# A gate with tokens on partitions, softmax divisions at the place of their transposes, a bias and a sum moved, in a streamed-weight transformer kernel

## Chip, core and metric
One core of one Trainium2 chip runs the whole kernel. The metric is the device time in microseconds (us) of one execution; the time before is the median of three runs.

## The reference
256 tokens with 1024 channels in float32 run through three kinds of block. First two layers of a mixing block and a feed-forward; the mixing block has four branches:

```
h = rms_norm(x, g_mix[l]);  proj = h @ w_in[l]
y_a = dsa_attention(qa, ka, va, qi, ki, iw) @ w_oa[l]      # softmax over the 64 best keys of an indexer
y_b = silu(layer_norm(causal_dwconv(glu))) @ w_ob[l]
y_c = (gb * causal_dwconv(gc * xc)) @ w_oc[l]
y_d = stick_breaking_attention(sq, sk, sv) @ w_od[l]
merged = gates[0] * y_a + gates[1] * y_b + gates[2] * y_c + gates[3] * y_d
x = x + merged @ w_merge[l]
x = x + (silu(causal_dwconv(h2 @ w_ffn_gate[l])) * (h2 @ w_ffn_up[l])) @ w_ffn_down[l]
```

Then two layers of a hybrid block, with latent attention (MLA, 4 heads), a gated delta rule (GDN, 4 heads of 128, chunks of 64) and block attention with a position bias (MoBA):

```
beta = sigmoid(b);  g = -exp(A_log) * softplus(a + dt_bias)      # b, a: 4 + 4 columns of the input product
gc = cumsum(g in a chunk);  decay = exp(gc_i - gc_j)
q, k, v = silu(causal_conv(qkv));  q, k normed
L = strict(beta * k k^T * decay);  W, U0 = (I + L)^-1 [k beta exp(gc), v beta]
A = q k^T * decay;  o = scan over chunks of the state
mla: softmax(q k^T + causal) v;  moba: softmax(q k^T * scale + t5_bias) v
```

and a last norm.

## The kernel before
Every engine runs a program written out by hand, in which a step waits on semaphores and raises one; `Values` keeps which count belongs to which value. Weights come in parts of 1024 columns by 128 partitions (four to a column group), streamed by one queue into `ring` (three slots). For each part ScalarE (ACT) writes the rounded high half `whi` (`split_hi`, L1250), VectorE (DVE) the low half `wlo` = weight - high (`split_lo`, L1884), and TensorE (PE) computes high times high, high times low halves (L525, L547, L614) and then low times high (L534, L555, L636). DVE and ACT split part j + 4 while PE is at part j. PSUM has eight banks; main products rotate over four ("m"), side products over the other four ("s"), and `Banks.take` waits until the previous owner's readers have left.

All else is side work. It is written as generators (`sparse_p`, `decay_v`, `delta_a` and so on: `_p` on PE, `_a` on ACT, `_v` on DVE) that are run at places of the tables MIX_PLAN and TWO_PLAN. Place 2j of a stage is, on PE, between the high and the low products of part j, and place 2j + 1 behind them; on ACT and DVE place 2j is ahead of the split of part j + 4, and 2j + 1 behind it. The stages in order: two layers of mixing and feed-forward, then the hybrid stage "two", layer 0 in about 969 to 1147 us, layer 1 from there to the end.

The parts that the change touches:
- Softmax: `logits_v` (masks and scales the products, L2001, maxima at L2005) waits for ACT's exponentials (L1316) and divides (L2008 reciprocal, L2010 product). PE then transposes the quotients (L504, `cst` is the identity), four blocks for token block 0 and eight for block 1. It runs for sparse attention in the mix layers, for MLA and for MoBA in the hybrid ones.
- The delta gate: `ba_p` multiplies the 8 gate columns (stationary, L896) with all 256 tokens; `ba_a` copies the 8 rows out of PSUM (L1615), `decay_p` transposes them, `decay_v` (L2446 to L2473) and `decay_a` (L1621 to L1640) make beta, the log decays, their sums and the decay matrix `Dm`. Ahead of the sums, `awake` puts six products of ones on PE (L499).
- The keys' convolution: `two_a` copies one half of the channel products (L1787), `two_v` adds the other (L2715), then `four_taps` (L2426) on DVE and ACT (L1780).
- The norm squares of keys and queries: ACT squares at L1704, and PE sums over channels (the x16 products with one column, L499 `onesb,w`).
- The queries' scores A, step 1 of `others`; T_, the update of the block solve of the delta rule, L2611 and L2616 on DVE, with Mm as its matrix buffer.
- The position bias: `bias_p`, four products with a flip matrix, and `bias_v`, copies and the causal mask, in layer 0 of the hybrid stage.
- MoBA's output neighbours: DVE's L2649 to L2656 norm the delta output and take their root from GpSimd (POOL, L2772).

Of the kernel before, what the change touches and what calls it, by code (L numbers as in the profile page):

```python
# [7 lines left out]
F32R = mybir.dt.float32r  # L8
# [5 lines left out]
P = 128  # L14
# [59 lines left out]
def two0(l):  # L74
# [14 lines left out]
        "stick": [100, 105, 107, 113],  # L89
# [92 lines left out]
def build(nc, a, out):  # L182
    ctx = ExitStack()
    with ctx:
# [23 lines left out]
        wba = sb("wba", [P, 64])  # L208
        bhi = sb("bhi", [P, 64], F32R)
        blo = sb("blo", [P, 64], F32R)  # L210
# [23 lines left out]
        def part2(o, n):  # L234
            return w2[:, o:o + n]
# [33 lines left out]
        def cols(h):  # L269
# [43 lines left out]
        rows8 = part2(23040, S)[0:8]  # L313
# [26 lines left out]
                                              bufH[:, 0:512]))  # L340
# [153 lines left out]
        def tensor(e):  # L494
# [108 lines left out]
            def chans_first(j, held_of, name, l, mid, after):  # L603
# [17 lines left out]
                for i in range(4):  # L621
# [5 lines left out]
                    products(i, 0, (2, 3))  # L627
                for i in range(4):
# [215 lines left out]
            def ffn_p(l):  # L844
# [35 lines left out]
            def bias_p(l):  # L880
                for h in range(4):
                    yield h
                    bk = ps.take(e, "s", "bias", h)
                    e.wait_ge(DMA["bi"], 64)
                    e.wait_ge(DMA["fl"], 16)
                    group(bk[:, 0:S], [(flipB, toepB[:, h * S:(h + 1) * S])]).then_inc(*up("bias.p"))
                    put("bias.p", "bias", h)

            def ba_p(l):
                yield 1  # L890
                bk = ps.take(e, "s", "ba", l)
                wh, wl = (b[:, :].rearrange("p (k n) -> p k n", k=8) for b in (bhi, blo))
                e.wait_ge(*at("ba", "lo", l))
# [4 lines left out]
                done.then_inc(*up("ba.p"))  # L898
                put("ba.p", "ba", "done", l)

            def decay_p(l):
                yield 0
# [2116 lines left out]
```

## Time and profile before
| | |
|---|---|
| time, median of three runs | 1321.51 us (1320.49 to 1323.34) |
| profiled execution | 1323.16 us, span 1321.4 us |
| PE busy | 1295.2 us, 98% |
| DVE busy | 1037.0 us, 78% |
| ACT busy | 734.9 us, 56% |
| POOL busy | 49.3 us, 4% |
| HBM read | 223.49 MB, 170 GB/s over the span |

The span runs from the first to the last instruction of one execution. A timeline row of the section of rows below gives the start in the span, the time the group took, the engine, the line, the operation, output and input by the program's names, the form of one, how many, and in brackets the engine's idle time ahead of it with what ended it. Where a group holds both an engine's and another's rows, the rows are of two timelines. Granted clock is TensorE's, as a share of full speed.

### The profile page before, as it was taken

The page shows a single profiled execution, that of the slowest core. Times are in us where ns is not written, and L with a number is a line of the kernel's source. Part 1 is how long each engine was busy: PE and PEld are TensorE (multiplying, and loading weights), DVE is VectorE, ACT ScalarE, POOL GpSimd, SP SyncE. Part 2 cuts the span into 40 slices and gives each one's busy share as a digit, 9 for nine tenths or more (in the row PEclk, how much of TensorE's full clock was granted, in tenths as well). Part 3 has the DMA queues.
Part 4 walks back from the last instruction along what each step waited for, and adds up shares of the span by engine and source line. Part 5 has one row for each costly group of instructions (what it writes and reads, how often), then busy time and mean ns, then how long its engine had stood idle before and what let it go on. Part 6 is the DMA issues. An engine that isn't in the chain of part 4 may idle for free.

```text
span 1321.4 us, 26181 instructions
## 1 busy us (share of the span) xinstructions
PE 1295.2 (98%) x10716; PEld 1233.1 (93%) x10716; DVE 1037.0 (78%) x1733; ACT 734.9 (56%) x1087; POOL 49.3 (4%) x48
## 2 busy tenths in 40 slices
PE   8999999999999999999999999999999999999998
PEld 8899999999999989999999999999989899898997
DVE  7999998678877677999997778777777846787565
ACT  6554566555454455544747565454557546585364
POOL 0000000000000000000000000000001100001100
PEclk9999999999999999999999999999999999999999
DMA  8565455565555457655355547665653224433232
GB/s 297 189 200 183 160 162 184 167 223 202 197 192 191 152 200 232 210 163 202 125 207 166 198 150 252 211 206 180 208 184 128 65 97 130 141 125 111 81 103 74
DMA packets 109711, 226.23 MB, mean 171 GB/s; under 512 B 6260, under 2 KB 17780, under 8 KB 109592
## 3 DMA queue, kind: packets, MB, share of 16 engines
q1 hardware_dynamic: 104656, 218.91, 49.6%
q10 hardware_dynamic: 4936, 5.65, 1.3%
q8 instruction: 85, 1.39, 0.4%
q14 instruction: 34, 0.28, 0.1%
HBM read 223.49 MB, written 1.06 MB: 170 GB/s over the span
## 4 chain that ended last, share of the span: by engine, by line
PE 78%; DVE 13%; ACT 3%; issue 3%; DMA 2%; POOL 0%; SPq 0%; POOLq 0%; DVEq 0%; ACTq 0%
PE bank L525 29%; PE bank L534 15%; PE bank L547 11%; PE bank L499 7%; PE bank L555 6%; DVE wlo L1884 4%; PE bank L586 3%; PE bank L504 2%; DMA ring<-in_w_in 2%; DVE w L2085 2%; PE bank L593 2%; DVE w L2426 1%; PE bank L614 1%; ACT whi L1250 1%; PE bank L636 1%
## 5 line engine op out<-in xcount | busy, mean ns | idle before, releaser
L1250 ACT ACTIVATE whi<-ring 128x1024 fp32r<-128x1024 f32 (+3 forms) x428 | 431.3, 1024 | 329.2 <-PE bank L525 194.9
L1884 DVE TENSOR_TENSOR wlo<-ring,whi 128x1024 fp32r<-128x1024 f32 (+3 forms) x428 | 495.8, 1184 | 147.9 <-ACT whi L1250 121.6
L525 PE MATMUL bank<-hboth,whi 128*128 128x256 f32 x3648 | 452.1, 277 | 1.3 <-DVE w L2715 1.3
L525 PEld LDWEIGHTS bank<-hboth,whi 128*128 128x128 f32 x3648 | 430.4, 193 | 3.6 <-issue 2.2
L534 PE MATMUL bank<-hboth,wlo 128*128 128x256 f32 x1824 | 247.4, 277 | 0.0
L534 PEld LDWEIGHTS bank<-hboth,wlo 128*128 128x128 f32 x1824 | 223.3, 192 | 3.8 <-issue 3.2
L547 PE MATMUL bank<-whi,hboth 128*128 128x512 f32 (+2 forms) x448 | 98.8, 363 | 0.0
L2085 DVE SCALAR_TENSOR_TENSOR w<-w,par 128x256 f32<-128x256 f32 x240 | 98.0, 478 | 0.0
L499 PE MATMUL bank<-w 64*64 64x64 f32 (+6 forms) x1312 | 88.3, 245 | 3.0 <-DVE w L2611 2.4
L547 PEld LDWEIGHTS bank<-whi,hboth 128*128 128x128 f32 x448 | 80.3, 189 | 9.3 <-issue 0.9
L499 PEld LDWEIGHTS bank<-w 64*64 64x64 f32 (+3 forms) x1312 | 73.6, 148 | 11.0 <-DVE w L2550 2.8
L2772 POOL TENSOR_TENSOR st<-st,mhalf 128x1 f32<-128x1 f32 (+2 forms) x34 | 36.2, 1064 | 1174.0 <-DVE st L1905 540.6
L614 PE MATMUL bank<-hboth,whi 128*128 128x256 f32 x384 | 52.2, 283 | 3.5 <-DVE hboth L1912 2.5
L547 PE MATMUL bank<-whi,fhi 128*128 128x512 f32 x144 | 54.6, 379 | 0.0
L547 PE MATMUL bank<-whi,flo 128*128 128x512 f32 x144 | 54.6, 379 | 0.0
L555 PE MATMUL bank<-wlo,hboth 128*128 128x512 f32 (+2 forms) x224 | 53.9, 363 | 0.0
L614 PEld LDWEIGHTS bank<-hboth,whi 128*128 128x128 f32 x384 | 47.0, 188 | 6.5 <-DVE hboth L1912 3.5
L555 PEld LDWEIGHTS bank<-wlo,hboth 128*128 128x128 f32 x224 | 40.7, 189 | 4.3
L1263 ACT ACTIVATE sgb<-x 128x512 f32<-128x512 f32 x28 | 17.6, 628 | 38.3 <-DVE x L1899 35.9
L1586 ACT ACTIVATE fhi<-w 128x512 fp32r<-128x512 f32 x22 | 13.9, 630 | 41.9 <-DVE w L2395 41.9
L555 PE MATMUL bank<-wlo,fhi 128*128 128x512 f32 x144 | 37.0, 379 | 0.0
L2382 DVE SCALAR_TENSOR_TENSOR w<-w,par 128x256 f32<-128x256 f32 x88 | 36.7, 478 | 0.0
(315 smaller groups left out, 1555.8 us busy)
## 6 DMA issues: line engine op xcount, KB each, us to landing
ring<-in_w_in SPq DMA_DIRECT2D x100, 1024.0 KB, 5.1
ring<-in_w_ffn_down SPq DMA_DIRECT2D x22, 1024.0 KB, 5.1
ring<-in_w_ffn_gate SPq DMA_DIRECT2D x20, 1024.0 KB, 5.1
ring<-in_w_ffn_up SPq DMA_DIRECT2D x20, 1024.0 KB, 5.1
ring<-in_w_merge SPq DMA_DIRECT2D x8, 1024.0 KB, 5.0
ring<-in_w_out SPq DMA_DIRECT2D x8, 1024.0 KB, 5.0
ring<-in_w_oc SPq DMA_DIRECT2D x4, 1024.0 KB, 5.2
ring<-in_w_od SPq DMA_DIRECT2D x4, 1024.0 KB, 5.1
```

Of the source, the lines that this page charges most:

```text
L499: done = e.matmul(o, l_, r_, start=start and i == 0, stop=stop and i == len(pairs) - 1)
L525: done = e.matmul(o, wh[:, k, cols(u)], paired(s_[:, k0 + k, :]), stop=False, skip_group_check=True, start=opens and k == 0 and s_ is sh a ...
L534: done = e.matmul(o, wl[:, k, cols(u)], paired(sh[:, k0 + k, :]), start=False, stop=closes, skip_group_check=True)
L547: done = e.matmul(held[u][:, 0:n], s_[:, k0 + k, cols(u)], paired(wh[:, k, 0:n]), stop=False, start=opens and k == 0 and s_ is sh, skip_gr ...
L555: done = e.matmul(held[u][:, 0:n], sh[:, k0 + k, cols(u)], paired(wl[:, k, 0:n]), start=False, stop=closes, skip_group_check=True)
L586: done = e.matmul(acc[nh][tb][:, :], s_[:, k0 + k, cols(tb)], paired(wh[:, k, :]), start=False, stop=False, skip_group_check=True)
L614: done = e.matmul(held[u][:, tb * S:tb * S + S], wh[:, k, cols(u)], hboth[:, :, 2 * i + k, cols(tb)], start=i == 0 and k == 0 and tb == 0, ...
L1250: e.activation(part_of(whi, j), part_raw(j), ACT.Copy).then_inc(*up("hi.a"))
L1884: e.tensor_tensor(part_of(wlo, j), part_raw(j), part_of(whi, j), ALU.subtract).then_inc(*up("lo.v"))
L2085: e.scalar_tensor_tensor(out=cacc[:, c], in0=glup[:, c, j:j + S], scalar=wv, in1=cacc[:, c], op0=ALU.mult, op1=ALU.add).then_inc(*up(name))
L2382: e.scalar_tensor_tensor(out=y, in0=g, scalar=wv, in1=y, op0=ALU.mult, op1=ALU.add).then_inc(*up("ffn.v"))
L2772: e.tensor_tensor(dst, src, half(n), ALU.pow).then_inc(*up(name))
```

## The change
Its parts:
1. The delta gate is computed with the tokens on partitions: `ba_products` uses the activations (128 tokens) as stationary and the 8 gate columns, high and low halves side by side in `bhl`, as moving side, 16 products for each token block. Block 0's run behind its first products of the keys' part, block 1's at place 5. DVE's `tensor_reduce` sums the parts straight out of PSUM. The copy of the rows, their transposes and the six idle products go. The decay's places are 5, 6, 7, 8, and the gate columns are split ahead of the norm.
2. The keys' high copy and sum are ahead of the split of the part that follows (`kc`, i == 3).
3. The position bias is computed in the last feed-forward, two banks and four DVE operations.
4. The division is a function `probs_v` of its own. Block 0's runs behind block 1's logits; block 1's at the place of PE's transposes: step 14 (place 146) for sparse attention, step 7 (place 41) for MLA, step 11 (place 63) for MoBA.
5. The queries' scores go from place 32 to 36; `Mm` has another buffer, and its wait for them goes.
6. Two steps of stick-breaking go from places 105 and 107 to 106 and 108.

```diff
-        "stick": [100, 105, 107, 113],
+        "stick": [100, 106, 108, 113],
...
-        "ba": [4, 7, 8],
-        "bias": [5, 5, 5, 6],
+        "ba": [5],
-        "others": [26, 32, 39, 39, 51],
-        "decay": [8, 8, 9, 10],
+        "others": [26, 36, 39, 39, 51],
+        "decay": [5, 6, 7, 8],
...
-                                              bufH[:, 0:512]))
+                                              big[:, 4 * S:6 * S]))
...
+                    if i6 == 0 and l == L - 1:
+                        bias_p()
...
+            def ba_products(l, tb):
+                if tb == 0:
+                    ps.take(e, "s", "ba", l)
+                    e.wait_ge(*at("ba", "lo", l))
+                bk = bank("ba", l)
+                for k in range(8):
+                    for s_, n in ((hhi, 16), (hlo, 8)):
+                        done = e.matmul(bk[:, 16 * tb:16 * tb + n], s_[:, k, cols(tb)], bhl[:, k, 0:n],
+                                        start=tb == 0 and k == 0 and s_ is hhi, stop=k == 7 and s_ is hlo, skip_group_check=True)
+                done.then_inc(*up("ba.p"))
+                put("ba.p", "ba", "done", l, tb)
...
-                for k in range(8):
-                    for w_, s_ in ((wh, hhi), (wh, hlo), (wl, hhi)):
-                        done = e.matmul(bk[0:8, 0:S], w_[:, k, :], paired(s_[:, k, :]), start=k == 0 and w_ is wh and s_ is hhi,
-                                        stop=k == 7 and w_ is wl)
...
-                for tb in range(2):
-                    done = turn(bk[:, 8 * tb:8 * tb + 8], rows8[:, cols(tb)])
...
-                awake(bk, 6)
...
-                chans_first(j, lambda u: ps.take(e, "m", name, l, u), "two", l, between, behind)
+                chans_first(j, lambda u: ps.take(e, "m", name, l, u), "two", l, between, behind,
+                            lambda: ba_products(l, 0))
...
-                e.activation(two(rows8), ordered(bank("ba", l)[0:8, 0:S])[:, 0], ACT.Copy).then_inc(*up("ba.a"))
...
-                yield 2
+                yield 3
                 e.wait_ge(*at("edl", "in", l))
...
-                    else:
-                        e.wait_ge(*at("A", l, 1))
...
+            def probs_v(name, l, tb, tag, lg, s0):
+                nk = P * (tb + 1)
+                g = heads(lg[tb])[:, :, 0:nk]
                 e.wait_ge(*at(tag, "exp", l, tb))
                 e.reciprocal(st[:, s0 + 8:s0 + 12], st[:, s0 + 4:s0 + 8]).then_inc(*up(name))
...
+                    if tb:
+                        probs_v(name, l, 0, "sparse", [A1, B1], 96)
+                yield 14
+                probs_v(name, l, 1, "sparse", [A1, B1], 112)
...
+                        if tb:
+                            probs_v(name, l, 0, tag, lgm, 96)
+                    yield 7 + 4 * i
+                    probs_v(name, l, 1, tag, lgm, 112)
...
-                e.tensor_copy(bg, blocks(bank("bg", l)[:, 0:16])).then_inc(*up(name))
+                e.tensor_reduce(bg, bank("ba", l)[:, 0:32].rearrange("p (t c n) -> p t n c", t=2, c=2), AX.X,
+                                ALU.add).then_inc(*up(name))
...
+                        if name == "kc" and i == 3:
+                            for c in range(4):
+                                g2 = two(gdp[:, c // 2, c % 2, 3:259])
+                                e.wait_ge(*at("kc_high", l, c))
+                                e.tensor_tensor(g2, g2, sides(bank(name, l, c))[1], ALU.add).then_inc(*up("two.v"))
+                                put("two.v", "kc_sum", l, c)
+                                leave("two.v", name, l, c)
+                            side.run(TWO_AT.get(2 * (j - two0(l)) + 1, ()))
                         split_to(j + 4)
```

How it moves instructions. Names: `bank` is PSUM, `st` small statistics, `w` work buffers, `sgb` the gates, `ring`, `whi`, `wlo` as above. DVE in the first mix layer, from the second block's logits on, before:

```order
L2001 SCALAR_TENSOR_TENSOR w<-bank,w 128x512 x2
L2005 TENSOR_REDUCE st<-w 128x4
L2008 RECIPROCAL st<-st 128x4
L2010 TENSOR_TENSOR w<-w,st 128x1024
L1884 TENSOR_TENSOR wlo<-ring,whi 128x1024 x2
L2340 TENSOR_TENSOR sgb<-bank,sgb 128x512
L2344 TENSOR_TENSOR w<-w,sgb 128x512
L2340 TENSOR_TENSOR sgb<-bank,sgb 128x512
L2344 TENSOR_TENSOR w<-w,sgb 128x512
L1884 TENSOR_TENSOR wlo<-ring,whi 128x1024 x3
```

and now:

```order
L1995 SCALAR_TENSOR_TENSOR w<-bank,w 128x512 x2
L1999 TENSOR_REDUCE st<-w 128x4
L2006 RECIPROCAL st<-st 128x4
L2008 TENSOR_TENSOR w<-w,st 128x4x128
L1878 TENSOR_TENSOR wlo<-ring,whi 128x1024 x2
L2342 TENSOR_TENSOR sgb<-bank,sgb 128x512
L2346 TENSOR_TENSOR w<-w,sgb 128x512
L2342 TENSOR_TENSOR sgb<-bank,sgb 128x512
L2346 TENSOR_TENSOR w<-w,sgb 128x512
L1878 TENSOR_TENSOR wlo<-ring,whi 128x1024
L2006 RECIPROCAL st<-st 128x4
L2008 TENSOR_TENSOR w<-w,st 128x1024
L1878 TENSOR_TENSOR wlo<-ring,whi 128x1024 x2
```

The first division went behind the second block's maxima, and the second behind two low halves, the four operations of the merge (L2342, L2346) and a third low half; PE's order is the same there (sixteen high products, twelve transposes, eight low products).

DVE in the first hybrid layer, ahead of MoBA's transposes, before:

```order
L1884 TENSOR_TENSOR wlo<-ring,whi 128x1024 x4
L2649 SCALAR_TENSOR_TENSOR st<-bank,st 128x8
L2653 TENSOR_SCALAR st<-st 128x8
L2656 TENSOR_TENSOR st<-st 128x8
L2662 SCALAR_TENSOR_TENSOR w<-w,par,bank 128x512
L2670 TENSOR_TENSOR w<-w 128x512
```

and now:

```order
L1878 TENSOR_TENSOR wlo<-ring,whi 128x1024 x4
L2657 SCALAR_TENSOR_TENSOR st<-bank,st 128x8
L2661 TENSOR_SCALAR st<-st 128x8
L2664 TENSOR_TENSOR st<-st 128x8
L2006 RECIPROCAL st<-st 128x4
L2008 TENSOR_TENSOR w<-w,st 128x1024
L2670 SCALAR_TENSOR_TENSOR w<-w,par,bank 128x512
L2678 TENSOR_TENSOR w<-w 128x512
```

Here the reciprocal and the product (L2006, L2008) stand between the delta norm's step on GpSimd's root (L2664) and the gated outputs.

ACT at the keys' part of the hybrid stage, before:

```order
L1250 ACTIVATE whi<-ring 128x1024 x2
L1787 ACTIVATE w<-bank 128x256 x4
L1780 ACTIVATE w<-w,par 128x256 x4
L1615 ACTIVATE w<-bank 8x256
L1621 ACT_TABLE_LOAD
L1621 ACTIVATE st<-par 128x4
L1623 ACTIVATE st<-st 128x8
L1625 ACTIVATE st<-st 128x8
L1627 ACTIVATE st<-st 128x8
L1629 ACT_TABLE_LOAD
L1629 ACTIVATE st<-st 128x8
L1250 ACTIVATE whi<-ring 128x832
```

and now:

```order
L1249 ACTIVATE whi<-ring 128x1024 x3
L1615 ACT_TABLE_LOAD
L1615 ACTIVATE st<-par 128x4
L1617 ACTIVATE st<-st 128x8
L1619 ACTIVATE st<-st 128x8
L1621 ACTIVATE st<-st 128x8
L1623 ACT_TABLE_LOAD
L1623 ACTIVATE st<-st 128x8
L1767 ACTIVATE w<-bank 128x256 x4
L1249 ACTIVATE whi<-ring 128x1024
L1778 ACTIVATE w<-w,par 128x256 x4
L1627 ACT_TABLE_LOAD
L1627 ACTIVATE st<-st 128x8
L1629 ACTIVATE st<-st 128x4
L1633 ACTIVATE w<-w 128x512 x2
L1249 ACTIVATE whi<-ring 128x832
```

The keys' copies (L1787, now L1767) went from ahead of the table loads of the gate to behind them, and the copy of the gate rows (L1615 before) is gone; the last of the seven full high halves is now behind the keys' copies, and the decay matrix's exponentials (L1633) ahead of the first narrow high half.

## Rows read from the trace of the kernel before
**Rows 1.** The page's first part: busy time, share of the span, instructions.
```profile
PE 1295.2 (98%) x10716; PEld 1233.1 (93%) x10716; DVE 1037.0 (78%) x1733; ACT 734.9 (56%) x1087; POOL 49.3 (4%) x48
```

**Rows 2.** PE's waits over the run: us in total, times, longest.
```profile
PE bank L499 <- DVE w L2611: 2.4, 2, 1.2
...
PE bank L770 <- ACT w L1416: 1.2, 1, 1.2
```

**Rows 3.** Timeline of PE, 224 to 227 (first mix layer, part 73).
```profile
224.41 1.84 PE L504 MATMUL bank<-cst,w 128*128 128x128 f32 x12
```

**Rows 4.** Timeline of DVE, 223 to 234 (same place).
```profile
223.66 0.18 DVE L2008 RECIPROCAL st<-st 128x4 f32<-128x4 f32 x1 [2.42 <-ACT w L1316]
...
225.01 2.35 DVE L1884 TENSOR_TENSOR wlo<-ring,whi 128x1024 fp32r<-128x1024 f32 x2
227.28 0.68 DVE L2340 TENSOR_TENSOR sgb<-bank,sgb 128x512 f32<-128x512 f32 x1
...
229.94 3.49 DVE L1884 TENSOR_TENSOR wlo<-ring,whi 128x1024 fp32r<-128x1024 f32 x3
```

**Rows 5.** Timeline of ACT, 223 to 227 (same place).
```profile
223.53 2.94 ACT L1250 ACTIVATE whi<-ring 128x1024 fp32r<-128x1024 f32 x3
```

**Rows 6.** Timelines of PE and DVE, 1117 to 1120 (MoBA, layer 0).
```profile
1117.23 1.51 PE L504 MATMUL bank<-cst,w 128*128 128x128 f32 x12
...
1119.53 0.17 DVE L2656 TENSOR_TENSOR st<-st 128x8 f32<-128x8 f32 x1 [1.75 <-POOL st L2772]
```

**Rows 7.** Timelines of PE and DVE, 1066 to 1069 (MLA, layer 0).
```profile
1066.97 1.53 PE L504 MATMUL bank<-cst,w 128*128 128x128 f32 x12
...
1066.26 0.69 DVE L1884 TENSOR_TENSOR wlo<-ring,whi 128x512 fp32r<-128x512 f32 x1
```

**Rows 8.** Timeline of ACT, hybrid stage: keys to squares, layer 0; last row layer 1.
```profile
979.56 2.00 ACT L1250 ACTIVATE whi<-ring 128x1024 fp32r<-128x1024 f32 x2 [3.41 <-DMA ring<-in_w_in]
981.47 1.19 ACT L1787 ACTIVATE w<-bank 128x256 f32<-128x256 f32 x4
...
1002.90 0.90 ACT L1250 ACTIVATE whi<-ring 128x832 fp32r<-128x832 f32 x1 [1.47 <-PE bank L525]
1003.79 0.60 ACT L1799 ACTIVATE w<-bank 128x512 f32<-128x512 f32 x1
...
1006.18 1.18 ACT L1704 ACTIVATE w<-w 128x512 f32<-128x512 f32 x2
...
1155.05 2.01 ACT L1250 ACTIVATE whi<-ring 128x1024 fp32r<-128x1024 f32 x2 [2.23 <-DMA ring<-in_w_in]
```

**Rows 9.** Timeline of DVE, same stretch, layer 0.
```profile
989.54 0.17 DVE L2450 TENSOR_TENSOR st<-st,par 128x8 f32<-128x8 f32 x1
...
992.04 0.17 DVE L2456 SCALAR_TENSOR_TENSOR st<-st 128x8 f32<-128x8 f32 x1
...
993.84 2.46 DVE L2426 SCALAR_TENSOR_TENSOR w<-w,par 128x256 f32<-128x256 f32 x6
996.21 0.69 DVE L2469 TENSOR_TENSOR w<-st,cst 128x512 f32<-128x512 f32 x1
...
998.49 0.69 DVE L2473 TENSOR_TENSOR w<-bank,w 128x512 f32<-128x512 f32 x1
```

**Rows 10.** Timeline of PE: bias and squares, layer 0; last row layer 1.
```profile
977.47 1.46 PE L499 MATMUL bank<-w 128*128 128x256 f32 x6
...
1006.99 1.92 PE L499 MATMUL bank<-onesb,w 128*128 128x1 f32 x16
...
1178.21 1.92 PE L499 MATMUL bank<-onesb,w 128*128 128x1 f32 x16
```

**Rows 11.** Windows: PE, PEld, DVE, ACT, POOL busy (count), granted clock, DMA, GB/s.
```profile
990.00:993.00 3.00, 1.55 (x15) 1.36 (x13) 0.71 (x3) 2.95 (x6) 0.00 (x0) 1.00 0.08 27
993.00:996.00 3.00, 3.00 (x17) 3.00 (x18) 2.96 (x9) 2.90 (x5) 0.00 (x0) 0.59 0.00 0
996.00:1000.00 4.00, 4.00 (x33) 4.00 (x33) 2.88 (x5) 3.53 (x6) 0.00 (x0) 0.88 0.00 0
```

More of the change, by code:

```diff
@@ L901, in decay_p, with bias_p @@
-            def decay_p(l):
-                yield 0
-                bk = ps.take(e, "s", "bg", l)
-                e.wait_ge(*at("rows8", l))
-                for tb in range(2):
-                    done = turn(bk[:, 8 * tb:8 * tb + 8], rows8[:, cols(tb)])
-                done.then_inc(*up("decay.p"))
-                put("decay.p", "bg", l)
+            def bias_p():
+                e.wait_ge(DMA["bi"], 64)
+                e.wait_ge(DMA["fl"], 16)
+                for i in range(2):
+                    bk = ps.take(e, "s", "bias", i)
+                    for h in (2 * i, 2 * i + 1):
+                        done = group(bk[:, (h % 2) * S:(h % 2) * S + S], [(flipB, toepB[:, h * S:(h + 1) * S])])
+                    done.then_inc(*up("bias.p"))
+                    put("bias.p", "bias", i)
@@ L1159, in two_p @@
                 j = two0(l)
-                side = Tasks(ba=ba_p(l), others=others_p(l), decay=decay_p(l), delta=delta_p(l), latent=latent_p(l),
-                             **({"bias": bias_p(l)} if l == 0 else {}))
+                side = Tasks(ba=ba_p(l), others=others_p(l), decay=decay_p(l), delta=delta_p(l), latent=latent_p(l))
                 def between(j):
@@ L1761, in two_a @@
                 j = two0(l)
-                side = Tasks(ba=ba_a(l), taps=taps_a(l), others=others_a(l), decay=decay_a(l), delta=delta_a(l), latent=latent_a(l),
+                side = Tasks(taps=taps_a(l), others=others_a(l), decay=decay_a(l), delta=delta_a(l), latent=latent_a(l),
                              outs=outs_a(l))
@@ L1771, in two_a @@
                         side.run(TWO_AT.get(2 * (j - two0(l)), ()))
+                        if name == "kc" and i == 3:
+                            e.wait_ge(*at(name, "done", l))
+                            e.wait_ge(*at("z4", l))
+                            for c in range(4):
+                                e.activation(two(gdp[:, c // 2, c % 2, 3:259]), sides(bank(name, l, c))[0],
+                                             ACT.Copy).then_inc(*up("two.a"))
+                                put("two.a", "kc_high", l, c)
                         split_to(j + 4)
@@ L1781, in last_tap @@
                                          scale=prm("gdn_w", l, wc, wc + 1)).then_inc(*up("two.a"))
-                        e.wait_ge(*at(name, "done", l))
-                        if name == "kc":
-                            e.wait_ge(*at("z4", l))
-                            for c in range(4):
-                                e.activation(two(gdp[:, c // 2, c % 2, 3:259]), sides(bank(name, l, c))[0],
-                                             ACT.Copy).then_inc(*up("two.a"))
-                                put("two.a", "kc_high", l, c)
+                        if name != "kc":
+                            e.wait_ge(*at(name, "done", l))
                         for i in range(2):
@@ L2701, in two_v @@
                 j = two0(l)
-                side = Tasks(ba=ba_v(l), taps=taps_v(l), others=others_v(l), decay=decay_v(l), delta=delta_v(l), latent=latent_v(l),
-                             outs=outs_v(l), **({"bias": bias_v(l)} if l == 0 else {}))
+                side = Tasks(taps=taps_v(l), others=others_v(l), decay=decay_v(l), delta=delta_v(l), latent=latent_v(l),
+                             outs=outs_v(l))
                 for name, _, _ in TWO_IN:
@@ L2707, in two_v @@
                         side.run(TWO_AT.get(2 * (j - two0(l)), ()))
+                        if name == "kc" and i == 3:
+                            for c in range(4):
+                                g2 = two(gdp[:, c // 2, c % 2, 3:259])
[4 more added lines that the diff above has]
+                            side.run(TWO_AT.get(2 * (j - two0(l)) + 1, ()))
                         split_to(j + 4)
```

73 lines of the change are left out of this document (26 added, 47 removed).

## Prediction
> **What bounds the kernel now.** The page's first part comes first: TensorE (PE) is busy for 98% of the span, so whatever makes PE wait, or gives it work, is nearly the whole story [rows 1]. Then the table of PE's waits: the ones this change touches are short, 2.4 us before the second product of the triangular solve and 1.2 us in the stick-breaking scores [rows 2]. So there is hardly a wait left to win, and the question is which new ones appear. For that I read the timelines of the three places where the order moves, engine by engine, and ask of each moved instruction what now stands ahead of it and when PE wants its result. The profiled execution took 1323.16 us, 1.65 above the median of the three runs; the sum is made against it and 1.65 is taken off at the end. A change under 0.2% (2.6 us) cannot be told from none here.
>
> **1. Sparse attention's second division (mix layers).** Before, VectorE (DVE) finished the second token block's logits, had its maxima, waited 2.42 us for the exponentials (from 221.24), and divided at once (223.66 to 225.01, 1.35 us for reciprocal and product) [rows 4]. PE came to the twelve transposes at 224.41; four are the first block's, so it wants the second block's quotient about 0.45 later, at 224.86, and met it nearly exactly [rows 3]. Now the order of DVE shows two low halves, four merge operations and a third low half between the exponentials and this division. The early part cannot be done while DVE waits for the exponentials: ScalarE (ACT) makes the high halves these low halves need only behind the exponentials, three in 2.94 us from 223.53 [rows 5]. So: first high half ready at 224.6, two low halves in 2.35, 226.95; the four merges 2.66 (227.28 to 229.94), 229.6; the third low half 3.49/3 = 1.16, 230.8; reciprocal and product 1.35, 232.15, and 0.1 to hand over [rows 4]. PE, whose order here is unchanged, stands from 224.86 to about 232.3: 7.4 us, in the middle of part 73, with its low products queued behind the transposes. Nothing is made up later, since every other engine has slack and PE has none. The same order stands in the second mix layer: **+14.8**. What the move frees is DVE's time 221.2 to 222.4, in which the first division now runs; nobody waited for it.
>
> **2. MoBA's second division (two-layers).** Before, PE ran the transposes from 1117.23. Now the division stands behind an instruction of the delta output's norm that waited until 1119.53 for GpSimd's root (1.75 us) [rows 6]. 1119.53 + 0.17 + 1.44 for reciprocal and product = 1121.1; PE wants it at 1117.23 + 0.42 = 1117.65. 3.5 us, in both layers: **+7.0**. Behind the division, the norm's next product waits for 16 PE instructions that come after the transposes, so it only moves back with PE.
>
> **3. MLA's second division, the solve, the queries' scores.** DVE wrote the solve's update until 1066.26, PE waited for it (the 2.4 us of [rows 2] over two layers). The division in front of it goes (1.35), but the low half in front is bound by ACT, so the update comes only some 0.4 earlier. Then DVE makes a narrow low half, 0.69 from 1066.26, and the division: 1065.9 + 0.69 + 1.35 = 1067.9. PE, 0.4 earlier too, would start its transposes at 1066.57 and want the second block 0.42 later, at 1067.0 [rows 7]. 0.9 late and 0.1 to hand over, less 0.4 gained: +0.6 each, **+1.2**. The queries' scores move four places later, with no bank or buffer wait added; PE takes 0.3 more in each layer by my reading of both orders, bounded by 0 and by the 1.2 us that one such wait reaches in [rows 2]: **+0.6**.
>
> **4. The gate, the keys' sum, the decay.** The start of the norm squares is where the reordered chain meets PE again. Before it was 1006.99 and 1178.21 [rows 10]. Followed through the new orders with old durations, layer 0: the seventh high half waits for its weights, a DMA, in both versions (979.56, first done at 980.6) [rows 8]. Low half 1.22, gate sums and bias 0.4: 982.2; from there to the finished gate 2.67 as from 989.54 to 992.21 [rows 9]: 984.9. ACT copies the keys (1.19, [rows 8]) to 985.5 beside DVE's last gate step, splits the eighth part (1.0), 986.5; its low half 1.2, 987.7, and DVE's taps of the keys 2.46: 990.1. The decay matrix, four operations from 996.21 to 999.2 with 0.3 of waits in it, 2.7: 992.8; its exponential 0.6, 993.4. High half 0.9, low half 0.9: 995.2; taps 2.4, 997.6; silu 0.6, 998.3; three high halves 2.6, 1000.9; the queries' copies 2.4 (1003.79 to 1006.18); first square 0.6 (half of 1.18): 1003.9 [rows 8, 9]. PE has less than this to do meanwhile. So layer 0 gains 3.1. In layer 1 the DMA lets the chain start at 1155.05 [rows 8], 175.5 later, which puts the squares at 1179.4 against 1178.21: 1.2 lost. Together **-1.9**. The chain is worked out over 15 steps; I give it 3 us either way per layer.
> The gate's own matmuls: the nearest row is 16 products with a one-column moving side in 1.92 us, some 110 ns each [rows 10], though they have 128-column stationaries just as the new ones do. 32 of them are 3.5 us a layer, against 24 wide ones and the six idle products that go. All lie in the stretch where PE waits for the chain, so **0**; with no cover the bounds are +1 and -3 a layer. The Trainium skill ("TensorE: Matmul & The Clock Gate", Wait — 56ns, not 53.3ns?) puts the floor between two starts at about 25 ns, by which the 32 would take 0.8 us and PE would merely stand longer before the gate; the sum stays as it is, the row decides.
>
> **5. The bias.** In the two-layer its products filled a stretch in which PE waits for that DMA anyway (six of them 1.46 us) [rows 10]; there its going gains nothing beside the chain. In the feed-forward PE has no such gap: 6 x 0.24 + 2 x 0.24 = **+1.9**. The four operations that DVE gets there are half its old eight, and it is idle 22% of the span [rows 1]; if that cover fails, they cost up to 2.4 us once (0.6 each, as its 512-wide operations).
>
> **6. Stick-breaking.** Two steps one place later remove the single wait of [rows 2]: **-1.2**.
>
> **7. The clock.** In the trace the granted clock fell to its lower level (1.2 GHz, half) for a few us after PE had idled: 0.59 in 993 to 996 and 0.88 in 996 to 1000, with PE having worked 1.55 of the 3 us before 993 [rows 11]. The cost is 0.41 x 3 + 0.12 x 4 = 1.7 us. Two stalls of 7.4 us are longer than any idle time PE now has, and two of 3.5 us stand at about the length that did it. I take both long ones and one of the short: 3 x 1.7 = **+5.1**; bounds 0 and 12 (twice at the long ones, each short one, and the gates, with some 1.7 each). The drop already in the two-layer stays hidden by the chain.
>
> Sum: 14.8 + 7.0 + 1.2 + 0.6 - 1.9 + 1.9 - 1.2 + 5.1 = 27.5; 1323.16 + 27.5 - 1.65 = **1349.0 us**, 2.1% slower.
>
> **The rivals.**
> *The divisions are in time (faster).* DVE may run far enough ahead of PE that place 146 is reached before PE gets to its transposes. It is ahead by up to four parts as the program is written, and it gets to the exponentials' wait earlier than before. Against it: the high halves come from 223.53 on, 2.35 + 2.66 + 1.16 stand before the division, and PE is there at 224.86 [rows 3 to 5]. It decides from less than 0.5 us of work between. Then terms 1, 2 and 7 go, the solve's whole wait (2.4) is won: 1323.16 - 1.9 + 1.9 - 1.2 - 2.4 + 0.6 - 1.65 = 1318.5. Chance 0.08; and 0.02 that the same case ends within 0.2%, since 1318.5 lies only 0.4 us past that bound.
> *Half a stall.* The merges do not stand in front in one layer, MoBA's root is ready earlier since GpSimd is asked sooner, or the clock does not fall: 1349 less 5.1, 7.0 or both, 1337 to 1344. For it: waits elsewhere shift, and the root's 1.75 us starts with an instruction that may move. Chance 0.15.
> *The clock falls more often.* Each of the long stalls has a second slow stretch behind it, and the idle stretch before the gate another: 3 to 5 more of 1.7, 1354 to 1358. Chance 0.12.
> *The gate gives nothing at all, or takes.* The chain's 15 steps are off by 3 us in both layers to the bad side: 1355. Contained in the last one's range; to the good side, 1343.
>
> **How the numbers follow.** The forecast itself, both long stalls, MoBA's and some clock loss (1344 to 1354): 0.63. With the half stalls and the frequent drops 0.90 is slower. Same 0.02, faster 0.08. The range runs from 1336, the lower end of the half stall, to 1358, the upper end of the clock's: what lies outside is the faster case and a tail of some 0.08.
>
> **What would show it.** Right: in PE's waits, the transposes (L501) released by the product of the division (L2008) with about 7 us twice, 3 to 4 us twice, and under 1 us twice; DVE's order of starts as worked out; the solve's wait (it was L2611) down from 2.4 to about 1.6; squares near 1004 plus the 17 or so us that the earlier stages lost; a granted clock near 0.5 for 3 us behind the long stalls. Wrong: no wait of PE on L2008 over 1 us (then the first rival); or the waits there but the span shorter than 1340, which would mean that PE makes time up that I think it cannot.

## The result, and the profile after

The changed kernel takes 1350.35 us (median of five runs, 1349.2 to 1353.74) against 1321.51 before: ratio 1.0215, 95% interval 1.0202 to 1.0227. The profiled execution took 1350.62 us, its span is 1348.8 us. The forecast was 1349.0, in 1336 to 1358.

The page of the changed kernel, its head and first part:

```profile
span 1348.8 us, 26143 instructions
## 1 busy us (share of the span) xinstructions
PE 1301.0 (96%) x10704; PEld 1240.6 (92%) x10704; DVE 1035.9 (77%) x1729; ACT 729.9 (54%) x1081; POOL 51.3 (4%) x48
```

PE has 5.8 us more busy time with twelve instructions fewer [rows 1], and its share fell by two points: of the 27.4 us of span 21.6 are idle time of PE, and the smaller part is work done slowly. PE's waits, longest total first (us in total, times, longest):

```profile
PE bank L501 <- DVE w L2008: 22.2, 6, 7.2
PE bank L496 <- DVE st L2460: 3.8, 2, 2.3
PE bank L496 <- ACT w L1697: 3.5, 2, 1.9
PE bank L501 <- DVE w L2512: 2.3, 2, 1.2
...
PE bank L501 <- ACT w L1420: 0.5, 1, 0.5
```

(L501 is the line of PE's transposes, L496 that of its small products, the norm squares among them.) The new first row is the transposes waiting for the division's product, six times, 22.2 us. The solve's row [rows 2] is gone, so is the stick-breaking wait of 1.2; one of 0.5 stands in its stage instead. The third row, L1697, is new in this length too: PE now reaches the norm squares ahead of ScalarE and stands 1.59 and 1.94 us there, where before it did not wait. In the first mix layer, VectorE (timeline, to compare with [rows 4]):

```profile
221.33 0.17 DVE L2006 RECIPROCAL st<-st 128x4 f32<-128x4 f32 x1
221.53 0.69 DVE L2008 TENSOR_TENSOR w<-w,st 128x512 f32<-128x512 f32 x1
224.78 2.36 DVE L1878 TENSOR_TENSOR wlo<-ring,whi 128x1024 fp32r<-128x1024 f32 x2 [2.55 <-ACT whi L1249]
227.05 0.69 DVE L2342 TENSOR_TENSOR sgb<-bank,sgb 128x512 f32<-128x512 f32 x1
...
229.71 1.22 DVE L1878 TENSOR_TENSOR wlo<-ring,whi 128x1024 fp32r<-128x1024 f32 x1
230.84 0.17 DVE L2006 RECIPROCAL st<-st 128x4 f32<-128x4 f32 x1
231.05 1.22 DVE L2008 TENSOR_TENSOR w<-w,st 128x1024 f32<-128x1024 f32 x1
```

The first division moved into time when VectorE had nothing to do, and VectorE still stood 2.55 us, now for ScalarE's high halves. Then came everything that is in front of the second division, and that ended at 232.27. PE at the same place, to compare with [rows 3]:

```profile
224.57 0.60 PE L501 MATMUL bank<-cst,w 128*128 128x128 f32 x4
232.33 1.97 PE L501 MATMUL bank<-cst,w 128*128 128x128 f32 x8 [7.15 <-DVE w L2008]
233.94 2.06 PE L531 MATMUL bank<-hboth,wlo 128*128 128x256 f32 x8
```

After the wait of 7.15 us the eight low products take 2.06 us. The same eight in the kernel before take 1.14:

```profile
226.00 1.14 PE L534 MATMUL bank<-hboth,wlo 128*128 128x256 f32 x8
```

The windows show why (PE, its loads, VectorE, ScalarE and GpSimd busy, granted clock, DMA share, GB/s):

```profile
228.00:231.00 3.00, 0.00 (x0) 0.00 (x0) 2.96 (x5) 0.00 (x0) 0.00 (x0) 0.50 0.91 277
231.00:234.00 3.00, 1.67 (x9) 1.68 (x9) 1.24 (x2) 0.52 (x1) 0.00 (x0) 0.50 0.19 72
234.00:237.00 3.00, 3.00 (x16) 3.00 (x15) 0.89 (x1) 1.62 (x3) 0.00 (x0) 0.50 0.00 0
237.00:240.00 3.00, 3.00 (x26) 3.00 (x25) 0.54 (x2) 1.06 (x1) 0.00 (x0) 0.90 0.43 95
```

The granted clock is at its lower level, half, and stays there for some 5 us after the transposes came. MoBA, first hybrid layer, VectorE and PE (two timelines, to compare with [rows 6]):

```profile
1136.53 0.17 DVE L2664 TENSOR_TENSOR st<-st 128x8 f32<-128x8 f32 x1 [1.75 <-POOL st L2782]
1136.62 0.17 DVE L2006 RECIPROCAL st<-st 128x4 f32<-128x4 f32 x1
1136.82 1.22 DVE L2008 TENSOR_TENSOR w<-w,st 128x1024 f32<-128x1024 f32 x1
...
1138.10 1.97 PE L501 MATMUL bank<-cst,w 128*128 128x128 f32 x8 [3.23 <-DVE w L2008]
```

Where the 27.4 us arose, by points that both traces have (the first products that wait for the second token block's `hboth`, the squares of the keys, the first products of a hybrid layer; each difference is what the stage added):

| stage | before | after | added | forecast |
|---|---|---|---|---|
| first mix layer, to its feed-forward | 316.69 | 326.39 | 9.70 | 7.9 |
| that feed-forward | 495.20 | 504.61 | -0.29 | 0 |
| second mix layer | 793.67 | 811.87 | 8.79 | 9.1 |
| its feed-forward, with the bias, to the hybrid stage | 966.12 | 986.04 | 1.72 | 1.9 |
| hybrid layer 0, to the squares | 1006.99 | 1023.50 | -3.41 | -3.1 |
| hybrid layer 0, rest | 1142.77 | 1165.19 | 5.91 | 5.2 |
| hybrid layer 1, to the squares | 1178.21 | 1201.78 | 1.15 | 1.2 |
| hybrid layer 1, rest | 1321.4 | 1348.8 | 3.83 | 5.2 |

(In the forecast column the clock's 5.1 is laid at 1.7 to each mix layer and half of that to each hybrid one.)

### The profile page after: what moved, and what is told of

Its sections match the earlier page's. It is cut to its first block, busy times and chain, and to the rows that moved or that the text cites. A ratio compares the mean times of both kernels' runs of the same rounds, so it can differ in the third digit from the quotient of the medians.

```text
span 1348.8 us, 26143 instructions
## 1 busy us (share of the span) xinstructions
PE 1301.0 (96%) x10704; PEld 1240.6 (92%) x10704; DVE 1035.9 (77%) x1729; ACT 729.9 (54%) x1081; POOL 51.3 (4%) x48
## 4 chain that ended last, share of the span: by engine, by line
PE 79%; DVE 13%; ACT 3%; issue 2%; DMA 2%; POOL 0%; SPq 0%; POOLq 0%; DVEq 0%; ACTq 0%
PE bank L522 29%; PE bank L531 15%; PE bank L544 12%; PE bank L496 7%; PE bank L552 6%; DVE wlo L1878 4%; PE bank L583 3%; PE bank L501 2%; DMA ring<-in_w_in 2%; DVE w L2083 2%; PE bank L590 2%; PE bank L611 1%; PE bank L635 1%; ACT whi L1249 1%; DVE w L2430 1%
## 5 line engine op out<-in xcount | busy, mean ns | idle before, releaser
L2083 DVE SCALAR_TENSOR_TENSOR w<-w,par 128x256 f32<-128x256 f32 x240 | 98.0, 480 | 0.0
L496 PE MATMUL bank<-w 64*64 64x64 f32 (+7 forms) x1312 | 88.4, 245 | 1.0 <-ACT w L1599 1.0
L496 PEld LDWEIGHTS bank<-w 64*64 64x64 f32 (+3 forms) x1312 | 73.9, 148 | 8.9 <-issue 1.3
L501 PE MATMUL bank<-cst,w 128*128 128x128 f32 (+1 forms) x180 | 28.4, 304 | 25.0 <-DVE w L2008 22.2
L501 PEld LDWEIGHTS bank<-cst,w 128*128 128x128 f32 (+1 forms) x180 | 22.3, 154 | 27.6 <-DVE w L2008 23.6
```

Source lines behind the costliest of these rows:

```text
L496: done = e.matmul(o, l_, r_, start=start and i == 0, stop=stop and i == len(pairs) - 1)
L501: return e.transpose(o, i_, ident[0:n, 0:n])
L2083: e.scalar_tensor_tensor(out=cacc[:, c], in0=glup[:, c, j:j + S], scalar=wv, in1=cacc[:, c], op0=ALU.mult, op1=ALU.add).then_inc(*up(name))
```

## The experiments

**The divisions alone.** The three pieces of `probs_v` put into the kernel before, nothing else:

```diff
+                    if tb:
+                        probs_v(name, l, 0, "sparse", [A1, B1], 96)
+                yield 14
+                probs_v(name, l, 1, "sparse", [A1, B1], 112)
...
+                        if tb:
+                            probs_v(name, l, 0, tag, lgm, 96)
+                    yield 7 + 4 * i
+                    probs_v(name, l, 1, tag, lgm, 112)
```

> The kernel before with nothing but the divisions moved as in the change. Theory: they carry the whole loss, 1321.5 + 26.7 = 1348 us, with six waits of PE on the product of the division. Rival (the gate, keys' sum, bias and clock carry a good part of it): under 1340 us.

Measured 1350.7 us (ratio to the kernel before 1.0216, 1.0194 to 1.0239), against 1350.35 for the whole change. Its waits:

```profile
PE bank L504 <- DVE w L2014: 22.2, 6, 7.2
...
PE bank L499 <- DVE w L2623: 1.6, 2, 0.8
```

The same 22.2 us. The divisions carry the whole loss, and the rest of the change comes to nothing. The second row is the solve: with nothing but the divisions moved its wait is down from 1.22 to 0.81 us in a layer.

**All else without the late divisions.** The other way round, the changed kernel with the second division straight behind the first:

```diff
                     if tb:
                         probs_v(name, l, 0, "sparse", [A1, B1], 96)
-                yield 14
-                probs_v(name, l, 1, "sparse", [A1, B1], 112)
+                        probs_v(name, l, 1, "sparse", [A1, B1], 112)
...
                             probs_v(name, l, 0, tag, lgm, 96)
-                    yield 7 + 4 * i
-                    probs_v(name, l, 1, tag, lgm, 112)
+                            probs_v(name, l, 1, tag, lgm, 112)
```

> The changed kernel with the second block's division straight behind the first's in all three attentions. Theory (the late divisions make PE wait 22.2 us in all, and the clock's slow stretches behind the long waits cost about 3.8 us in the mix layers and 3.1 in MoBA, while MLA's late place gains about 0.5 a layer): 1350.35 - 14.3 - 3.8 - 6.5 - 3.1 + 1.0 = 1323.7 us. Rival (DVE is late anyway; the wait moves to the low halves behind the division, L531 waiting for L1878): at least half of it comes back, 1335 us or more.

Measured 1322.59 us (ratio 1.0003, 0.9992 to 1.0013). The wait on the division is gone, and nothing took its place: the low halves' row is 1.4 us (1.5 in the change). The rival falls. One thing got worse than before, the clock. As a measure of what it costs, take each window of 3 us and multiply PE's busy time in it by the part of full speed that was not granted. Summed over the span this loss is 6.8 us here, most of it behind the squares of the hybrid stage, and 3.4 in the kernel before, in one profiled execution of each.

**MoBA early, the others late.** The same with `if i == 1` for the second half, sparse attention as changed.

> The changed kernel with MoBA's second division straight behind its logits, the others late. Theory: the two waits of 3.2 us and the slow clock behind each (about 1.5) go, 1350.35 - 9.6 = 1340.7 us. Rival A (the clock falls there for another reason, the idle time of the two-layer's start): only 6.5 comes back, 1343.9. Rival B (the root from GpSimd is what PE waits for in the end): under 2 us comes back, 1348.5 or more.

Measured 1342.05 us (1.0148, 1.0130 to 1.0166), 8.3 us less than the change, where 9.6 were expected and rival A, without the clock, had 6.5. The row on the division fell from 22.2 in six to 15.7 in four, that is by 6.5. The other 1.8 us are no wider than this run's interval, so the time alone hardly rejects rival A. The traces do: behind MoBA's transposes the granted clock is 0.50 and 0.64 in 1137 to 1143 and 0.56 in 1317 to 1320 in the change, and 1.00 in both layers here. Rival B falls.

**A dose.** If what stands ahead on VectorE sets the wait, taking out part of it must take out as much. The division at a place of its own, behind the two low halves and ahead of the merge (MoBA early):

```diff
+        "parts": [143],
...
-                yield 14
-                probs_v(name, l, 1, "sparse", [A1, B1], 112)
+            def parts_v(l):
+                yield 0
+                probs_v("parts.v", l, 1, "sparse", [A1, B1], 112)
```

> The changed kernel with MoBA's division early, and sparse attention's second division behind the two low halves but ahead of the merge's four operations and the third low half. Theory (what stands in front on VectorE sets the wait, term by term): the wait falls from 7.15 by 2.66 + 1.14 to about 3.3 us in both layers; against the run with MoBA early and sparse late (1342.05), 7.7 less for the waits and about 1 less for the clock, 1333.4 us. Rival (PE's own order or the bank's readers set the wait): it stays over 6 us and the time over 1340.

Measured 1334.73 us (1.0099, 1.0085 to 1.0113), so the rival falls. VectorE and PE, two timelines:

```profile
224.72 2.36 DVE L1879 TENSOR_TENSOR wlo<-ring,whi 128x1024 fp32r<-128x1024 f32 x2 [2.56 <-ACT whi L1250]
227.00 0.17 DVE L2007 RECIPROCAL st<-st 128x4 f32<-128x4 f32 x1
227.20 1.22 DVE L2009 TENSOR_TENSOR w<-w,st 128x1024 f32<-128x1024 f32 x1
...
228.48 1.97 PE L502 MATMUL bank<-cst,w 128*128 128x128 f32 x8 [3.36 <-DVE w L2009]
```

The wait is 3.36 us in both layers, forecast 3.3, so the five instructions taken out of its front were 3.8 us of it. The time is 7.3 us under the MoBA run (6.5 by the two ratios), 8.7 expected. The eight low products behind the wait take 2.06 us in the first layer, as in the full stall, and 1.81 in the second (2.06 in the full stall), so the shorter wait hardly spared the slow clock.

**The clock.** PE kept busy in the wait, with products of ones ahead of the second block's transposes in the changed kernel. First with too many:

```diff
+                        if tb and not kb:
+                            awake(bk, {"sparse": 58, "mla": 2, "moba": 24}[tag])
+                            e.wait_ge(*at(tag, "probs", l, tb))
```

> The changed kernel with products of ones (58 for sparse attention, 24 for MoBA, 2 for MLA, about 0.12 us each by the twelve in 1.50 us of the kernel before) on PE while it waits for the second block's division. Theory (the slow stretches behind the waits come of PE's idling): same waits in length, but the granted clock stays near 1.0 behind them, and 6.5 to 7 us come back, 1343.5 us. Rival A (the clock falls for another reason): 1350 us and the same slow windows. Rival B (the products overrun the wait or take bank time): 1352 us or more.

Measured 1359.41 us (1.0279, 1.0263 to 1.0295): rival B. One call of `awake` in float32 is two matmuls, which the kernel's own twelve for six had shown:

```profile
224.80 13.12 PE L496 MATMUL bank<-onesb 128*128 128x128 f32 x116
```

116 of them took 13.12 us, and PE overran a wait of 7; behind them the eight low products take 1.14 us, at full clock. So half as many (28, 12 and 2):

> The changed kernel with half the products of ones of the run before (28 for sparse attention, 12 for MoBA, 2 for MLA; each is two matmuls of 0.11 us in the trace), so that they end inside PE's waits of 7.2 and 3.2 us. Theory (the slow stretches behind the waits come of PE's idling): the granted clock stays near 1.0 behind them, and the division still comes when it did, so about 6 us come back, 1344 us. Rival (the clock falls whatever PE does in the wait): 1350 us.

Measured 1344.04 us (1.0169, 1.0155 to 1.0183), 6.3 us under the change, with the division as late as before (PE meets it at 232.11, in the change at 232.33). PE's timeline and the windows:

```profile
224.79 6.42 PE L496 MATMUL bank<-onesb 128*128 128x128 f32 x56
232.11 1.09 PE L501 MATMUL bank<-cst,w 128*128 128x128 f32 x8 [0.90 <-DVE w L2012]
232.96 1.14 PE L531 MATMUL bank<-hboth,wlo 128*128 128x256 f32 x8
```

```profile
228.00:231.00 3.00, 3.00 (x29) 3.00 (x28) 2.93 (x6) 0.00 (x0) 0.00 (x0) 1.00 0.96 309
231.00:234.00 3.00, 2.10 (x19) 1.91 (x19) 1.05 (x1) 1.20 (x3) 0.00 (x0) 1.00 0.13 46
234.00:237.00 3.00, 3.00 (x29) 3.00 (x29) 1.23 (x1) 1.87 (x2) 0.00 (x0) 1.00 0.00 0
```

The eight low products are back at 1.14 us, and the clock is at 1.00 behind all four waits, so the rival falls. PE's idling in the waits cost some 6 us beyond the waits. The figure is not quite that alone: by the windows this run lost 3.3 us to the lower clock and the change 13.4, of which 8.2 behind the four waits and 5.1 in three stretches of the hybrid stage, where this run happens to have one of 3.3.

**MLA's place, and the queries' scores.** Sparse attention and MoBA early, MLA late as in the change:

> The changed kernel with the second division early in sparse attention and MoBA, late in MLA as in the change. Theory (late, it costs PE a wait of 0.7 a layer in MLA but takes away the solve's wait of 1.2): 0.5 a layer less than with all three early, 1322.6 - 1.1 = 1321.5 us. Rival (as forecast, the late place costs 0.6 a layer): 1323.8 us.

Measured 1322.74 us (1.0012, 1.0003 to 1.0020), neither of the two and, within what these runs tell, the same as with all early (1322.59). The traces are finer: PE waits 0.72 us for the division in a layer and not for the solve, where with all early it waits 0.40 for the solve. So the late place costs 0.3 a layer. Then the queries' scores back at their old place, all divisions early:

```diff
-        "others": [26, 36, 39, 39, 51],
+        "others": [26, 32, 39, 39, 51],
```

> The kernel with all three divisions early (1322.59), the queries' scores back at place 32 (the solve's buffer stays the new one). Theory (their move, not the division's, took 0.8 us a layer off the solve's wait, which is 0.4 with all divisions early): the wait on L2621 is back at about 1.2 each and the time 1 to 1.6 us more, 1324 us. Rival (as forecast, the scores' move costs PE 0.3 a layer and the solve's wait came down through the divisions): 0.6 less, 1322.0 us, and the wait stays 0.4.

Measured 1323.93 us (1.0015, 1.0004 to 1.0026), 1.3 more, with intervals that overlap; what follows rests on the traces. PE at the solve, in this kernel:

```profile
1066.15 1.15 PE L496 MATMUL bank<-w 64*64 64x64 f32 x32 [1.22 <-DVE w L2621]
```

and with the scores late (all divisions early):

```profile
1065.01 1.15 PE L496 MATMUL bank<-w 64*64 64x64 f32 x32 [0.40 <-DVE w L2621]
```

So the scores' move took 0.8 us a layer off the solve, and the division's, by the run with the divisions alone, the other 0.4: together the whole wait of 1.22. The row L501 waiting for L2512 rose from 1.6 (0.8 each) to 2.3 by the same move, in all runs that have it: 0.4 of each 0.8 is given back there, in MLA's rotation.

**Stick-breaking.** On the kernel with the two divisions early:

```diff
-        "stick": [100, 106, 108, 113],
+        "stick": [100, 105, 107, 113],
```

> The kernel with sparse attention's and MoBA's divisions early, stick-breaking's two steps back at places 105 and 107. Theory (the wait of 1.2 us was taken away, but waits of 0.5 and 0.6 us came behind it in the same stage): the old places cost under 0.3 us either way. Rival (as forecast): 1.2 us more.

Measured 1323.67 us (1.0016, 1.0008 to 1.0025), 0.9 more, between the two, and the intervals overlap. Its trace has the wait of 1.2 back. In exchange the 0.5 us on L1420's values is gone, and the low halves' row is 0.7 instead of 1.5 in all. Summed, these waits are 1.9 us with the old places and 2.0 with the new, so the move took nothing off them; the time does not settle more.

**The bias.** On the same kernel, the bias back in the hybrid stage, but at other places than before: PE's products behind the gate's second block, VectorE's four operations where it waits for the softplus.

```diff
-                    if i6 == 0 and l == L - 1:
-                        bias_p()
...
                 ba_products(l, 1)
+                if l == 0:
+                    bias_p()
...
                 put(name, "t4a", l)
+                if l == 0:
+                    bias_v()
```

> The kernel with sparse attention's and MoBA's divisions early, and the bias (eight products on PE, four operations on DVE) back in layer 0 of the hybrid stage: PE's at place 5 behind the gate's second block, DVE's between the gate's sum and the wait for its softplus. Theory (the feed-forward pays 1.8 us for it and PE waits 1.9 to 2.3 us ahead of the decay's sums anyway): 1.5 us less than the same kernel with the bias in the feed-forward. Rival (the keys' copies wait for PE's products and the chain to the squares moves back by as much): no difference, within 0.5 us.

Measured 1321.64 us (1.0006, 0.9995 to 1.0016), 1.1 less than with the bias in the feed-forward (1322.74), the intervals overlapping. By the traces the hybrid stage began at 966.23 instead of 967.81, and the squares of its layer 0 came at 1004.15 instead of 1005.34: 1.6 won in the feed-forward, 0.4 paid in the gap.

**The gate's products twice.**

```diff
+                        done = e.matmul(bk[:, 64 + 16 * tb:64 + 16 * tb + n], s_[:, k, cols(tb)], bhl[:, k, 0:n],
+                                        start=False, stop=k == 7 and s_ is hlo, skip_group_check=True)
```

> The kernel with both divisions early (1322.74), and every gate product issued twice, the second into columns that nobody reads: 32 more products with 8 or 16 moving columns a layer. Theory (about 0.11 us each, in a stretch where PE waits for the chain on VectorE and ScalarE): 16 in 1.84 us again; the first block's 16 delay the keys' products by 1.7 but mostly into idle time ahead of the decay's sums; 0 to 1.5 us more in all, 1322.7 to 1324.2. Rival (nothing hides them): 2 x 32 x 0.11 = 7.0 us more, 1329.7.

Measured 1333.48 us (1.0097, 1.0081 to 1.0112): 10.7 us more than the 1322.74 of its base, worse than the theory and the rival. The cover ended. VectorE's gate sum, which came straight behind a low half before, now waits for the second block's products:

```profile
987.60 0.19 DVE L2450 TENSOR_REDUCE st<-bank 128x16 f32<-128x32 f32 x1 [2.01 <-PE bank L901]
```

In the changed kernel PE ended those products at 1000.26 and the sum started at 1001.54: 1.3 us of slack, not the 2.3 of PE's wait further on. And the clock fell, as the windows show, with PE busy all the time:

```profile
972.00:975.00 3.00, 3.00 (x29) 3.00 (x29) 2.73 (x4) 1.09 (x2) 0.00 (x0) 1.00 0.31 43
975.00:978.00 3.00, 3.00 (x28) 3.00 (x28) 1.76 (x4) 0.00 (x0) 0.00 (x0) 0.96 0.97 346
978.00:981.00 3.00, 3.00 (x16) 3.00 (x16) 1.23 (x1) 1.06 (x1) 0.00 (x0) 0.50 1.04 404
```

Behind 32 products with 8 or 16 moving columns, from 973.3 to 976.8, the clock fell to half without any idle time of PE. It did so at all four such groups of the run, and in the base, with 16 in a group, the windows behind them stay at 1.00. No run separates the two, but the two profiles' pages give the sum. PE is busy 1307.6 us against 1293.5 in the base, 14.1 more, and idle 2.8 less. The 64 products more are 64 x 0.115 = 7.4 us of that, and the other 6.7 are slow work: by the windows this run lost 13.7 us to the lower clock, its base 6.8.

**A version that beats both.** The kernel with both divisions early and the bias in the gap, and the decay matrix one place later:

```diff
-        "decay": [5, 6, 7, 8],
+        "decay": [5, 6, 7, 9],
```

> The kernel with both divisions early and the bias in the hybrid layer's gap (1321.64), the decay matrix's step at place 9 instead of 8, so that ScalarE splits the next part while VectorE makes the matrix. Theory (ScalarE stands 1.87 us for the matrix ahead of that split, and this chain sets the squares): squares about 1 us earlier in each layer, 1319.6 us. Rival (the queries' taps and the silu behind the matrix are the chain): squares later, 1322 us or more.

Measured 1317.14 us (1316.29 to 1317.25, five runs), ratio to before 0.9966 (0.9954 to 0.9979): 0.3% faster than the kernel before and 2.5% faster than the changed one. Its page, and ScalarE where it had stood for the matrix ahead of the split:

```profile
span 1314.8 us, 26143 instructions
...
PE 1289.9 (98%) x10704; PEld 1230.6 (94%) x10704; DVE 1035.3 (79%) x1729; ACT 728.6 (55%) x1081; POOL 51.2 (4%) x48
```

```profile
985.55 1.72 ACT L1778 ACTIVATE w<-w,par 128x256 f32<-128x256 f32 x4
987.14 0.90 ACT L1249 ACTIVATE whi<-ring 128x832 fp32r<-128x832 f32 x1
988.07 1.28 ACT L1627 ACT_TABLE_LOAD   x1
```

The narrow high half now goes first. From the squares of layer 0 to those of layer 1 it is 171.15 us where the kernel without this step has 174.46, and up to the squares of layer 0 1.9 less; I had expected 1 us each. What is the step's own can be read on ScalarE: from the start of the keys' copies to the first square it takes 18.76 us in both layers without the step, and 17.28 and 17.27 with it. That is 1.5 us a layer. The other 1.5 us of the 4.5 were not separated by a run. By the traces they are the clock (5.1 us lost by the windows without the step, 3.4 with it) and, in layer 0, 0.4 us from weights that had arrived sooner, ahead of the step. The clock's slow windows between the decay's sums and the squares, in layer 1 of the run without the step, are gone; those behind the squares remain.

## Why the prediction was right

**Sparse attention (term 1), +14.8.** Right by its own steps: PE's wait was forecast at 7.4 and measured at 7.15, in both layers; the division's end was forecast at 232.15 and measured at 232.27. Two waits make 14.3. That VectorE cannot use its time at 221 to 224, because ScalarE's high halves come only from 223.5 on, is the wait of 2.55 in the trace. The dose and the two halves of the change show the cause.

**MoBA (term 2), +7.0.** 3.23 measured for 3.5, twice, so 6.5; MoBA early takes away just these 6.5 us of waits.

**MLA, the solve, the scores (term 3), +1.8.** Wrong in its sum and in its sign. One step held: the division's going brings the solve's update 0.4 earlier (1.22 to 0.81 with the divisions alone). The division itself then cost a wait of 0.72 where 1.0 was forecast, so late it costs 0.3 a layer and not 0.6. The step that failed is the queries' scores, forecast to cost PE 0.3 a layer: their move brought the solve 0.8 earlier, with 0.4 of that lost in the rotation. Together about -0.2 in two layers instead of +1.8. I had worked out when PE meets the scores and not what their operations on VectorE stood in front of.

**Gate, keys' sum, decay (term 4), -1.9.** The squares: -3.41 and +1.15, forecast -3.1 and +1.2. That PE "has less than this to do" up to the squares held: it waits 1.59 and 1.94 us there. But behind the squares more windows were slow than before (with all divisions early 6.8 us lost in the run, 3.4 before), which the forecast did not have. The gate's products took 1.84 us for 16, as the row of one-column products had it (1.92 for 16). The Trainium skill ("TensorE: Matmul & The Clock Gate", Wait — 56ns, not 53.3ns?) gives about 25 ns as the least between two starts, by which 16 would take 0.4 us, an estimate. These products stay far above that floor, so something else sets their pace, and no run here shows what. They were hidden as said, but by a cover of 1.3 us, and the bound that I gave for its going (+1 a layer) was too small: doubled, they cost 10.7 us in two layers.

**The bias (term 5), +1.9.** 1.72 measured up to the hybrid stage.

**Stick-breaking (term 6), -1.2.** The step "removes the single wait" was right, its worth not: a wait that ends shows the next one, 0.5 and 0.8 us behind it. No gain can be seen at the end of this stage.

**The clock (term 7), +5.1.** 6.3 by the run with PE kept busy. It fell behind all four long waits, MoBA's two included, of which I had taken one. The reason that I gave for taking one was a misreading: ahead of the fall at 993 [rows 11] PE had idled 1.45 us in one piece (3.00 less 1.55), not about 3.5, and the same wait of 1.45 us in layer 1 had no slow window behind it. The 1.7 us by windows was too small a price behind the first long wait: there the lower clock lasted 5 us of PE's work, which is some 2.5.

**The sum.** The measured parts are 14.3 + 6.5 - 0.2 - 2.3 + 1.7 + 0 + 6.3 = 26.3, against a span that grew by 27.4; 1.1 us has no owner. The two great terms and the mechanism are right. That the total came out at 27.4 for 27.5 is in part luck: terms 1 to 5 were some 3.6 us too high together, terms 6 and 7 came 2.4 us too low, and the 1.1 us without an owner do the rest.

Of the rivals, the one on the other side, the divisions in time, fell with 22.2 us of waits; its sum of 1318.5 for everything else was 4 us too low by the run that shows it (1322.59), since of the solve's 2.4 us only 1.6 came back, 0.7 of it went into the row on L2512, and stick-breaking's 1.2 did not come. The hybrid stage's longer slow stretches are in that gap too.

## What to carry to other kernels

A step moved "to where its result is wanted" in a hand-ordered program is not late by its own duration but by everything that the new place puts ahead of it on its engine, and what is ahead may itself start late for another engine's sake: add the row of instructions from the moment the slowest input arrives, and compare with when the waiting engine comes. On PE, which is 98% busy here, long new waits cost more than their length: four waits of 3.2 to 7.2 us, 20.8 in all, cost some 6 us more through the clock. Harmless products of 128 columns put into them took that surcharge away, as long as they ended inside the wait. A cost hidden in a gap is hidden up to the slack of the first consumer (1.3 us here), not up to the length of the next wait (2.3).

## What the runs showed of the hardware

Products with 128 stationary columns and 8 to 16 moving ones take 115 ns each in a row (16 in 1.84 us), as the one-column ones do. So do the filler's with 128 moving columns (116 in 13.12 us, 113 ns each): narrowing the moving side below 128 bought nothing here. At the lower clock the narrow ones take some 0.21 us each (from 1165.5 on in the run with the gate products twice).

The granted clock falls without idle time too: in that run, behind each of the four groups of 32 such narrow products. The stretch that stays in the best version also begins some 2 to 3 us after a group of 16 one-column products, the squares, and there a wait of 1.9 stands ahead. The kernel before has a case without that wait, in layer 1, with only 0.22 us of idle time ahead of the 16:

```profile
1191.95 1.92 PE L499 MATMUL bank<-onesb,w 128*128 128x1 f32 x16 [0.22 <-ACT w L1704]
```

```profile
1191.00:1194.00 3.00, 2.78 (x25) 2.62 (x24) 2.17 (x7) 2.27 (x4) 0.69 (x1) 1.00 1.04 401
1194.00:1197.00 3.00, 3.00 (x20) 3.00 (x20) 2.09 (x4) 1.21 (x3) 1.63 (x1) 0.65 0.34 128
```

So the long wait is not needed for it. Nor are the 16 enough: the same group in layer 0, at 1020.75 behind 0.23 us of idle time, has no slow window behind it. A wait of 3.36 us was enough for nearly the same slow stretch as one of 7.15 (eight low products 2.06 us in both in the first layer, 1.14 at the full clock).
